# Attention: which step of the next head pair carries the last value products, and when the results are copied out

## The reference, cut to what matters

```
for blk in range(S // Q_BLOCK):                       # 8 row blocks of 128 queries
    s = (q_nope @ k_nope[:, :q1] + q_rope @ k_rope[:, :q1]) * scale   # keys up to the block's end
    s = where(k_chunk <= q_chunk, s, -inf)            # chunks of 64
    prob = softmax(s)
    outs.append(prob @ v[:, :q1])
```

## Time and profile before

| what | value |
|---|---|
| median of 3 runs | 2052.22 us (2052.01 to 2052.26) |
| the profiled execution | 2051.6 us, its span from first to last instruction 2049.9 us |
| PE busy | 1922.3 us, 94% of the span |
| DVE, ACT, POOL busy | 782.4, 669.2 and 614.1 us |
| mean granted clock of PE | 0.979 |
| attention | from about 266 to 538 us of the span |

### The profile page before, as it was taken

One profiled execution on the slowest core, in us unless ns is written; L12 is line 12 of the kernel. 1 busy time (PEld: TensorE's weight loads), 2 busy tenths in 40 slices (PEclk: granted clock), 3 DMA queues, 4 the chain that ended last, 5 costly groups with the idle time before them and its releaser, 6 DMA issues. The chain is left out here.

```text
span 2049.9 us, 31303 instructions
## 1 busy us (share of the span) xinstructions
PE 1922.3 (94%) x11958; PEld 1361.9 (66%) x11958; DVE 782.4 (38%) x1437; ACT 669.2 (33%) x1486; POOL 614.1 (30%) x658
## 2 busy tenths in 40 slices
PE   7999999999999999999999989999989889798896
PEld 7998878787787777888887767767653233233232
DVE  5224256666553554440112356656521121111114
ACT  5334145555323344331122333333213222222222
POOL 2236387342120110001104576656212122122110
PEclk9999999999999999999999999999999899999988
DMA  7204451211321146523342422121389999999998
GB/s 255 96 32 175 135 195 27 52 27 47 144 72 39 42 80 118 102 54 97 104 103 93 173 82 74 63 73 47 123 348 417 425 425 424 425 424 425 424 424 359
DMA packets 103114, 371.39 MB, mean 181 GB/s; under 512 B 18752, under 2 KB 41664, under 8 KB 76096
## 3 DMA queue, kind: packets, MB, share of 16 engines
q1 hardware_dynamic: 85088, 327.32, 44.3%
q0 software_dynamic: 16704, 42.10, 5.4%
q10 hardware_dynamic: 1184, 0.04, 0.0%
HBM read 325.24 MB, written 60.95 MB: 188 GB/s over the span
## 5 line engine op out<-in xcount | busy, mean ns | idle before, releaser
L2880 PE MATMUL ps<-w_gu,rows_t 128*64 128x512 f32 x1024 | 241.0, 626 | 22.1 <-DMA w_gu<-w_up 20.5
L2880 PEld LDWEIGHTS ps<-w_gu,rows_t 128*64 128x64 f32 x1024 | 74.7, 144 | 163.7 <-issue 140.8
L2899 PE MATMUL ps<-w_d,act_tt 128*64 128x512 f32 x512 | 126.7, 640 | 25.2 <-DMA w_d<-w_down 24.6
L3175 POOL DMA_INDIRECT y_d<-y_out,asg_i x32 | 32.4, 1012 | 368.9 <-DVE y_out L2984 349.4
L2323 PE MATMUL ps<-w_o,mix_t 128*128 128x512 f32 x256 | 123.1, 609 | 0.0
L2975 DVE SCALAR_TENSOR_TENSOR act_g<-ps,rs_c,act_g 128x256 f32<-128x256 f32 x32 | 15.5, 483 | 278.7 <-ACT act_g L2966 278.7
L1110 ACT ACTIVATE prob<-ps,stats 128x1024 f32<-128x1024 f32 (+7 forms) x128 | 94.4, 738 | 62.7 <-DVE stats L1073 62.3
L322 PE MATMUL ps<-tk_lo,h_hi 128*128 128x512 f32 x256 | 99.9, 390 | 0.0
L322 PE MATMUL ps<-tk_hi,h_hi 128*128 128x512 f32 x256 | 99.7, 389 | 0.0
L322 PE MATMUL ps<-tk_hi,h_lo 128*128 128x512 f32 x256 | 99.7, 389 | 0.0
L1073 DVE TENSOR_REDUCE stats<-ps 128x1 f32<-128x1024 f32 (+7 forms) x128 | 97.0, 757 | 4.7 <-DVE ps L1071 0.3
(11 more groups left out here) (481 smaller groups left out, 4429.9 us busy)
## 6 DMA issues: line engine op xcount, KB each, us to landing
w_gu<-w_gate SPq DMA_DIRECT2D x64, 1024.0 KB, 23.5
w_gu<-w_up SPq DMA_DIRECT2D x64, 1024.0 KB, 25.9
w_d<-w_down SPq DMA_DIRECT2D x64, 1024.0 KB, 21.4
w_tk<-w_in SPq DMA_DIRECT2D x5, 2048.0 KB, 17.3
proj_d<-tok_o POOLq DMA_DIRECT2D x40, 256.0 KB, 2.3
tk_in<-proj_d SPq DMA_DIRECT2D x8, 1280.0 KB, 6.0
w_ch<-w_in SPq DMA_DIRECT2D x12, 512.0 KB, 9.1
proj_d<-conv_o POOLq DMA_DIRECT2D x12, 512.0 KB, 4.0
```

The source lines that it names most:

```text
L2880: mm = pe.matmul(ps[half, 2, :].rearrange("p (g n) -> p g n", g=2), rows_t[:, k, half], w_gu[q][:, h, :, k, :], start=(k == 0), stop=(k == ...
L2899: mm = pe.matmul(ps[half, 4 + j, :], act_tt[:, k, half], w_d[q][:, h, k, j * BANK:(j + 1) * BANK], start=(k == 0), stop=(k == 1))
L3175: pool.indirect_dma_start(out=y_d, out_offset=bass.IndirectOffsetOnAxis(ap=idx, axis=0), in_=y_out[q][:, :], in_offset=None, bounds_check= ...
```

## The change

V4 of the pair before moves from the end of slot 2 to slot 4, between the scores and the transposes. V0 moves from the end of slot 4 to slot 6, again between the scores and the transposes. Both copies of the results move from slot 3 to slot 5; on ACT they still stand ahead of the slot's other work, on DVE behind it. What follows the last pair is as it was. PE's order from slot 2 becomes

```diff
@@ att_pe @@
             def slot(u, p, j, prev):
                 if j < NJ:
                     scores(u, p, j)
+                if j == 4 and prev:
+                    values(u - 1, T - 1)
+                if j == 6:
+                    values(u, 0)
                 x = back(u, j, 2, prev)
                 if x and x[1] < NJ:
                     turn(*x)
                 x = back(u, j, 4, prev)
-                if x and x[1] % 2 == 0:
+                if x and x[1] % 2 == 0 and j not in (2, 4):
                     values(x[0], x[1] // 2)
@@ att_dve @@
-                if j % NJ == 3 and (prev or j > NJ):
+                if j == 5 and prev or j == NJ + 3:
                     outputs(v, done, 1)
```

## The result

The changed kernel has a median of 2054.45 us over 22 executions, against 2051.36 for the kernel before over as many: the ratio is 1.0015 with a 95% interval of 1.0009 to 1.0021, so it is slower by 1.8 to 4.3 us. The forecast was 2.4 us more, at 2054.6.

A forecast was written before the change was run, and what follows sets the result against it. PE, 97% busy, bounds the attention. Stalls of 1.57 replace 1.30: 0.27 a pair, 1.9 over seven, plus 0.48 in the first, 2.4; 2051.6 + 2.4 = 2054.0, plus 0.6 for the median, 2054.6 us; range 2050.5 to 2058.5.

The forecast's parts named there:

- The sum: Over the attention: 0.27 us lost in each of seven pairs, 1.9, plus 0.48 in the first pair, 2.4 us slower.
- S4's stand: Before S4, PE waits 1.35 us a pair for step 2's exponentials to free bank 2, no longer covered by V4.
- The old stalls: PE's waits in T2 (0.35) and at T3 (0.95), 1.30 us a pair, were to shrink to 0.22.
- The wait in T2: Mid-T2 wait for bank 5, behind ACT's copy of the results: 0.35 us a pair, forecast to go.
- the stall at T3: Between S5 and T3, PE's wait for a DVE copy: forecast 0.22 us a pair instead of 0.95.
- V0 without cover: In slot 6, V0 stands between S6 and V7 with nothing to hide it: 0.48 us a pair, passage included.
- The passages from scores to values: PE's change from scores to value products, twice a pair: 0.11 us each, bounds 0 and 0.29; upper-bound rival shares 0.16 chance.
- a full drain: At 14 new passages, a tiling change draining TensorE would add 0.06 us each, 0.8 in all, giving 2055.4.
- The copy of the results as a wait: Slower rival, slot 5: ACT's copy delays V0 beyond 0.57 us spare; 4.4 us more, 2059.0; chance 0.16 shared with passages.
- The clock: Slower rival: a longer PE stand lowers its clock, two microseconds at half speed a pair, 7.0 us, 2061.6; chance 0.03.
- The pair: One pair of the attention was to take about 34.05 us, where it took 33.79 before.

The follow-up runs named there:

- a kernel with the same stand: The changed kernel with V0 moved behind T4, right before V7: +1.3 us against the kernel before, ratio 1.0007 (0.9998 to 1.0016).

## Why the prediction was right, point by point

The sum was 2.4 us; the stage shows 2.8 (from S2 of the first pair to the last V4, 266.65 to 536.50 before and 267.20 to 539.85 after), and the executions 3.1, with an interval that holds both. The median came to 2054.45 for a forecast of 2054.6, and so near it is by luck: the loss was 0.7 short, and the three executions that it was added to had a median 0.9 above that of all 22.

- *S4's stand.* Predicted 1.35, measured 407.18 - 405.75 = 1.43 (T1's 405.65 and 0.10). T1 is through a little earlier than I had it, because S3 follows T0 in 0.03 where I took 0.10. That the chain and not PE's arrival opens S4 was argued from the first pair; V4 in slot 3 and the doubled maxima show it.
- *The old stalls.* The wait in T2 is gone as forecast, and the stall at T3 is 0.68 - 0.46 = 0.22, the number forecast. S6 gained 0.19 where I had 0.21.
- *V0 without cover.* 0.48 forecast, 2.14 - 1.63 = 0.51 measured; moved alone it cost 0.50 to 0.54 a pair, and the first pair lost 33.13 - 32.62 = 0.51, from its S2 to the next pair's.
- *The passages from scores to values.* Taken as 0.11, bounded by 0 and 0.29; measured 0.11 in front of V4 (407.74 - 407.18, less 0.45) and 0.08 in front of V0 (412.73 - 411.33, less S6's 1.32). The 0.06 more for a full drain did not show.
- *The copy of the results as a wait.* It had 0.57 to spare in my count and has 0.69.
- *The clock.* Not in the changed kernel's two profiles, so it does not carry the 2.8 us that the stage shows; the executions without a profile leave it open. But I gave it too little room: it happened once in a kernel with the same stand.
- *The pair.* 34.05 forecast, 34.11 measured.

What I did not see is how much was there to be had: V4 in front of S4 is one place earlier than the change put it, and turns +3.1 into -4.0. The balance of stalls also hides which move costs: V0's cover, lost, is 0.50 a pair, and the rest of the change gives 0.18 back.

## What to carry to other kernels

Before moving work off a busy engine's path, ask what latency that work covers: V4 looked like a load in slot 2 and was the cover of a chain of 4.4 us, from S2's start through DVE and ACT. A stall moved to a fixed wait is not a stall removed; here the gain lay in putting the piece exactly into the wait, one place earlier in the queue. A small piece like V0 was free only in a gap, and cost its passages too elsewhere, so put such pieces beside work of the same kind or into a stall. And take a change of several moves apart: the stand at S4 is the most visible one, but the stalls that went paid for it, and the loss came with V0.

## What the runs showed of the hardware that was not expected

A stand of PE of 1.4 to 1.5 us was followed, in one of 28 cases (21 at S4, seven at T3), by a granted clock of 0.50 for some three microseconds, at a loss of 1.6 us; one lengthened to 2.1 us in the first pair and 2.6 in the others was so in four of eight, in every second pair, for a loss of 0.8 us in the first and 1.3 in the others. The Trainium skill (TensorE: Matmul & The Clock Gate, Part 1) has the slow level as the default that activity releases, which these rows agree with. In both falls shown, S4, which ends the stand, still ran at 1.00, and the clock fell in the microsecond in which V4 began (0.65 and 0.93).

A change between products that fill 128 columns and those that fill 64 costs 0.08 to 0.11 us on the way in, behind scores as behind transposes, and 0.16 to 0.17 back (V4's 1.24 less 1.07 for its 20 instructions, V0's 0.37 less 0.21 for its 4); removing one such change each way a pair gave 0.30 back.
